# A product of 8 by 8 columns ahead of each unit that streams 256 tokens

## What is computed

```python
for l in range(2):      # first block
    h = h + 0.5 * swiglu_ffn(rms_norm(h, g1[l]), w1_in[l], w1_out[l])
    h = h + hybrid_mixer(rms_norm(h, gm[l]), ...)      # stick-breaking heads || gated delta rule
    h = h + memory_cross_attention(rms_norm(h, gx[l]), rms_norm(mem, gmem[l]), ...)
    h = h + 0.5 * swiglu_ffn(rms_norm(h, g2[l]), w2_in[l], w2_out[l])
h = rms_norm(h, g_final)
for l in range(2):      # second block, own weights
    x = x + 0.5 * swiglu(rmsnorm(x, ...), ...)
    q, k, v of three mixers, gate_logits = split(rmsnorm(x, ...) @ w_in[l])
    branches = einsum('bsnw,nwd->bsnd', [mixer_a, mixer_b, mixer_c], w_branch[l])
    x = x + sum(sigmoid(gate_logits) * branches) @ w_out[l]
    x = x + 0.5 * swiglu(rmsnorm(x, ...), ...)
return rmsnorm(x, ...)
```

## Time and profile before

| | |
|---|---|
| three runs | 2601.97, 2603.65, 2604.84 us |
| span of the profiled execution | 2604.7 us; it has no other time of its own |
| PE busy | 2573.5 us (99%), 14942 products |
| PEld busy | 2254.8 us (87%) |
| DVE, ACT, POOL busy | 1499.3 (58%), 1372.2 (53%), 272.3 us (10%) |
| weight loads | 792 of 512 KB, 3.3 us to landing |

### The profile page before, as it was taken

One profiled execution on the slowest core, in us unless ns is written; L12 is line 12 of the kernel. 1 busy time (PEld: TensorE's weight loads), 2 busy tenths in 40 slices (PEclk: granted clock), 3 DMA queues, 4 the chain that ended last, 5 costly groups with the idle time before them and its releaser, 6 DMA issues.

```text
span 2604.7 us, 39404 instructions
## 1 busy us (share of the span) xinstructions
PE 2573.5 (99%) x14942; PEld 2254.8 (87%) x14942; DVE 1499.3 (58%) x2034; ACT 1372.2 (53%) x2157; POOL 272.3 (10%) x180
## 2 busy tenths in 40 slices
PE   9999999999999999999999999999999999999998
PEld 7889999888888899898888879998888888999887
DVE  5558646555555774555556556457555555556654
ACT  5547445544544663655445445555445445565543
POOL 0200211000000002200100000552000000344000
PEclk9999999999999999999999999999999999999999
DMA  6555314455555541347755555335555555334554
GB/s 246 191 184 171 103 66 138 142 190 186 202 186 186 171 154 57 105 138 205 204 189 182 186 178 170 114 114 186 186 186 186 186 187 176 131 106 164 191 186 138
DMA packets 118348, 427.54 MB, mean 164 GB/s; under 512 B 13164, under 2 KB 14956, under 8 KB 117804
## 3 DMA queue, kind: packets, MB, share of 16 engines
q1 hardware_dynamic: 117696, 424.82, 49.2%
q10 hardware_dynamic: 492, 0.46, 0.1%
HBM read 423.79 MB, written 1.44 MB: 163 GB/s over the span
## 4 chain that ended last, share of the span: by engine, by line
PE 90%; DVE 5%; ACT 2%; issue 1%; DMA 1%; DVEq 0%; SPq 0%; POOL 0%; ACTq 0%; POOLq 0%
PE bank L482 74%; DVE lo_slots L470 2%; PE bank L990 2%; PE bank L1658 2%; PE bank L502 2%; PE bank L678 1%; PE bank L1697 1%; DMA raw<-w_full 1%; ACT hi_slots L456 1%; PE bank L1150 1%; PE bank L1674 1%; PE bank L624 1%; PE bank L1161 1%; PE bank L1159 1%; DVE conv_out L952 1%
## 5 line engine op out<-in xcount | busy, mean ns | idle before, releaser
L470 DVE TENSOR_TENSOR lo_slots<-raw,hi_slots 128x1024 fp32r<-128x1024 f32 x732 | 899.9, 1234 | 730.8 <-ACT hi_slots L456 730.7
L456 ACT ACTIVATE hi_slots<-raw 128x1024 fp32r<-128x1024 f32 x788 | 830.5, 1057 | 666.9 <-PE bank L482 647.4
L482 PE MATMUL bank<-hi_slots,x_hi_room 128*128 128x512 f32 x1536 | 608.9, 396 | 2.1 <-DVE x_lo_room L654 1.6
L482 PE MATMUL bank<-hi_slots,x_lo_room 128*128 128x512 f32 x1536 | 600.2, 391 | 0.0
L482 PE MATMUL bank<-lo_slots,x_hi_room 128*128 128x512 f32 x1536 | 599.2, 390 | 0.0
L482 PEld LDWEIGHTS bank<-hi_slots,x_lo_room 128*128 128x128 f32 x1536 | 288.9, 188 | 61.7
L482 PEld LDWEIGHTS bank<-hi_slots,x_hi_room 128*128 128x128 f32 x1536 | 289.1, 188 | 61.4 <-issue 4.2
L482 PEld LDWEIGHTS bank<-lo_slots,x_hi_room 128*128 128x128 f32 x1536 | 289.4, 188 | 57.3
L482 PE MATMUL bank<-x_hi_room,hi_slots 128*128 128x256 f32 x1152 | 331.8, 288 | 3.5 <-DVE x_lo_room L654 1.9
L482 PE MATMUL bank<-x_hi_room,lo_slots 128*128 128x256 f32 x1152 | 320.8, 278 | 0.0
L482 PE MATMUL bank<-x_lo_room,hi_slots 128*128 128x256 f32 x1152 | 320.8, 278 | 0.0
(11 more groups left out here) (330 smaller groups left out, 3145.8 us busy)
## 6 DMA issues: line engine op xcount, KB each, us to landing
raw<-w_full SPq DMA_DIRECT2D x792, 512.0 KB, 3.3
bias_mem<-bias_rows SPq DMA_DIRECT2D x8, 288.0 KB, 6.6
mem<-mem_t SPq DMA_DIRECT2D x2, 1024.0 KB, 8.1
const<-consts SPq DMA_DIRECT2D x1, 1664.0 KB, 8.6
h<-x_t SPq DMA_DIRECT2D x2, 512.0 KB, 7.6
final<-finals SPq DMA_DIRECT2D x2, 512.0 KB, 7.8
out_t<-h SPq DMA_DIRECT2D x4, 256.0 KB, 2.6
bias_rows<-junk ACTq DMA_DIRECT2D x1, 384.0 KB
```

What stands on the lines that cost most here:

```text
L456: nc.scalar.activation(w_hi[s], raw[s][:, :], ACT.Copy).then_inc(hi_ready[s], 1)
L470: nc.vector.tensor_tensor(w_lo[s], raw[s][:, :], w_hi[s].bitcast(F32), ALU.subtract).then_inc(lo_ready[s], 1)
L482: mm = nc.tensor.matmul(out, lhsT=a, rhs=b, start=start and n == 0, stop=stop and n == len(passes) - 1)
```

## The change

Ahead of every touched unit PE makes one more product: the first 8 tokens' columns of the first tile of normed tokens are the stationary operand, the first 8 columns of the unit's high weights stream, and the 8 x 8 result goes into the corner of the bank that the unit's own first product, which starts a new sum, overwrites. The operands and the bank are ones that the unit's waits have already made ready. In a lead it stands once, behind the wait for the first tile.

```diff
+        def narrow(out, x, w):
+
+            nc.tensor.matmul(out[0:8, 0:8], lhsT=x[:, 0, 0:8], rhs=w[:, 0:8], start=True, stop=True)
+
         def token_pair(first, xh, xl, outs, tiles=range(TT)):
@@ pe_lead
             for k in range(KT):
                 part(k)
+                if k == 0:
+                    narrow(bank[0], xh, w_hi[E.mid(group) % SLOTS])
                 for s in range(LEAD):
@@ pe_block
             pe.wait_ge(bank_free[s], E.evac(ev) + it)
+            narrow(bank[s], xh, w_hi[u % SLOTS])
             feature_block(u % SLOTS, xh, xl, bank[s][:, 0:TOK]).then_inc(block_done[u % SLOTS], 1)
@@ pe_gate
             pe.wait_ge(bank_free[before % SLOTS], E.evac(5 + before // SLOTS) + 1)
+            narrow(bank[2 + g % 2], xm_hi, w_hi[u % SLOTS])
             feature_block(u % SLOTS, xm_hi, xm_lo, bank[2 + g % 2][:, 0:TOK]).then_inc(block_done[u % SLOTS], 1)
@@ pe_branch_unit
             pe.wait_ge(bank_free[b], used)
+            narrow(bank[b], y_hi[:, 4 * n:4 * n + 1, :], w_hi[u % SLOTS])
             for j in range(2):
```

## The result

The changed kernel takes 2620.53 us (median of four runs, 2617.95 to 2622.65) against 2603.59 for the kernel before beside it (2601.97 to 2604.84). The ratio is 1.0064, 95% interval 1.0050 to 1.0079: slower by 13 to 21 us. The forecast was 2610.0 with a range up to 2619.5. The sign was right, but the cost, 17 us, is over twice the 6.3 us of the sum, and the time lies just above the range. The profiled execution took 2619.44 us, its span is 2617.7.

A forecast was written before the change was run, and what follows sets the result against it. PE was taken as the bound, 90% of the span; first block 2.8, cross attention 1.1 and second block 2.4 made 6.3 us, from span 2604.7 to 2611.0, 2610 for the median, range 2603 to 2619.5.

The forecast's parts named there:

- What bounds the kernel, and where: Whole kernel: PE's chain is 90% of the span; time is lost where products stand wider apart or PE waits.
- The 8-column load: At each narrow product: its load lies beside the 256 columns before it, cost 0.
- the 8-column product: At each of 162 places: the narrow product itself takes 6 ns on PE.
- The load behind it: Behind each narrow product: the 128-column load is bare, so the unit's first product ends 0.23 us after the short one.
- third rival: All seams: the load hides and slow units turn fast, -8.3 us, 2595.3; chance 0.13.
- The pace behind it: Every changed unit: fast from its second product on, 2.84 us; fast units lose 0.115, slow ones 0.01.
- first rival: All places: the pace is not set by the change, slow units stay slow and pay the load, 15.3 us; chance 0.17.
- The sum by stage: Whole kernel: 2.8 for projection with groups 4 and 5, 1.1 cross attention, 2.4 second block, together 6.3 us.
- Projection, gross: First block, projection with groups 4 and 5: 23 fast places a layer at 0.115, 5.3 us in both layers before cover.
- Cover: First block: delay hidden under PE's existing waits, 1.6 us in layer 0 and 2 x 0.45 at group 5, 2.5 together.
- Cross attention: Per layer: one lead, two fast units, one slow, three late to the fast pace, 0.56 us, nothing covered.
- Second block: Per layer: lead -0.10, 40 slow units 0.4, 10 fast places 0.9, together 1.2 us, no cover counted.

The follow-up runs named there:

- e9: The changed kernel with narrow products kept only in the first block of the mixers, 60 places: 2611.80 us, ratio 1.0028.
- e10: The changed kernel with narrow products kept only in the second block, 102 places: 2612.18 us, ratio 1.0032.
- e3: The changed kernel with the narrow product issued twice at each of the 162 places: 2619.69 us.
- e8: The changed kernel with 128 stationary columns in place of 8 in the narrow product, 8 moving: 2623.22 us.

## Why the prediction was wrong, by its own steps

*What bounds the kernel, and where:* right. What was added on PE came out in the time, the blocks add up (e9, e10).

*The 8-column load* at cost 0 and *the 8-column product* at 6 ns: right as far as the rows can tell. The load is recorded at 0.09 beside the product before it; the narrow product takes 0.01 of the chain. Its own price can't be separated from that of the load behind it: from the last product of the unit before to the end of the first it is 229 ns (median) with 8, 16, 32 and 64 columns alike.

*The load behind it,* 0.23 from the last short product to the end of the first: right, measured 0.22, and the same in e3 and e8. The third rival (the load hides) is excluded by these 0.22 at the seams, where it had 0.12. The rule of the Trainium skill in "TensorE: Matmul & The Clock Gate", section "Architectural detail: the array is 16× 32×32, not 1× 128×128", that a product can begin while part of the array still loads, brought nothing for a load of full width here. The same page, section "Back-to-back issue gap", gives products of 1 to 64 columns one common gap of about 25 ns from start to start. The trace agrees: from the recorded start of the narrow product to the next start it is 27 or 28 ns (median) for 8, 16, 32 and 64 columns, although the product that starts then has to wait for its load and ends late.

*The pace behind it:* this is the step that failed. One unit (370.02, behind sixteen 1-column products) was taken as the model of all 162, all fast. In the changed kernel 95 are slow. A slow one is 2.94 where the sum had 2.84, so 95 x 0.10 = 9.5 us are missing; 6.3 + 9.5 = 15.8, against 14 to 17 measured. Without cover and idle times the comparison is closer: 8.8 + 9.5 = 18.3, against 17.8 in the trace, and e8 gives the same 0.11 for each slow unit more. The first rival (slow units stay slow), which was put at 15.3 us, came near in time, but its mechanism is half the story: three in four of attention's slow units do stay slow, while half of the branch units turn fast, and half of the projection's fast units turn slow, which no case of the prediction had. Its premise was that a fast unit stays fast behind a bare load. The model itself doesn't even hold for its own place: with one narrow product behind the sixteen 1-column products, the unit at 1761.35 is slow (2.93).

*The sum by stage.* Projection, gross: 3.3 a layer where 19 x 0.115 = 2.2 was forecast; 0.115 a place was right, the rest is half the units turned slow. Cover: 2.5 hidden was forecast; in layer 0 the lag fell by 2.0 over the two stalls, with four more places hidden in each layer, some 3 in all; but 0.9 of that is a stall that other executions lose without any narrow product. Cross attention: 1.14 a layer where 0.56 was forecast, the lead and three of the units being slow. Second block: 3.8 and 3.7 where 1.2 a layer was forecast; attention alone is 2.2, most of it 18 units of 2.83 that become 2.94. No cover was counted there, and there was a little, 0.3 a layer at the wait for the weight split.

*The range.* It ended at the centre of the first rival plus little. Had the unknown pace been taken at its other end for all places, 162 x 0.10 more than the sum, the bound would have been 2626, and the result inside. The prediction called this the point on which 84 places hang; it was 162.

*Smaller errors,* which don't move the forecast: the rows between 1630.64 and 1748.09 hold 23 units of 2.83, not 22. The ends 2607.5 and 2612.5 don't come out of the terms named for them, which give about 2608.6 and 2611.8. And the span of 2604.7 was set beside times, though a span is 1.8 below its time.

What stays open is what the pace is. Shown is that it is decided at a seam, holds to the end of the unit and over seams without a narrow product, and that the number, the width and the stationary side of the products in between turn it. It was the same in two executions of the changed kernel for 151 of 168 units; of the other 17, ten stand behind a wait. No run here measures what sets it, and no row tells the kinds of slow unit apart.

## What to carry to other kernels

When a trace shows one form of instruction at two paces, an edit at the seam between them can draw the pace anew everywhere, in both directions; price it for all places it touches, not only for those that could gain, and don't take one unit as the model. A product put on a full PE costs its seam, 0.115 here, whether its columns are 8 or 64; a unit that it turns fast gives back 0.108, so it pays only ahead of a run of several that it turns, as in the branches (5 units, 0.42). Then look at what the run ends in: at group 3 the same gain went into the next wait for DVE.

## What was not expected of the hardware

- Products of 128 x 128 by 256 columns in fp32r run at 113.3 or 117.7 ns at the same granted clock, 1.00. A product of 8 to 40 columns between two units turns a fast unit's successor slow (237 of 237), one of 48 to 96 doesn't (0 of 108), one of 128 does again (3 of 3).
- A longer insertion can be cheaper than a shorter one. In the projection's loop a unit takes 2.85 us with 64 columns ahead of it and 2.88 with two products of 8, but 2.89 in the mean with one of 8.
- The same product with 128 stationary columns in place of 8 costs no more at the seam (232 ns in place of 229), but leaves 137 of 162 units slow in place of 95.
